# The alignment of the moving tiles against the weight tiles, modulo 512 bytes

## What is computed

```python
def first_block(x, ...):                   # 256 tokens
    h = h + rglru_mixer(rmsnorm(h, ...))   # linear recurrence, width 1280
    h = h + conv_ffn(rmsnorm(h, ...))      # 1024 -> 2 x 3072 -> 1024
    h = h + nsa_mixer(rmsnorm(h, ...))     # sparse attention, 16 heads
    h = h + conv_ffn(rmsnorm(h, ...))
    return rmsnorm(h, final_norm_g)

def second_block(x, c, ctx, ...):          # layer 0: x and ctx, layer 1: x alone
    for l in range(2):
        h = modulate(rmsnorm_2(x, norm1_g[l]), sh1, sc1)
        ...  = split_in(h @ w_in[l])
        x = x + g1 * merge(br_a, br_b, br_c, gates, w_out[l])
        x = x + g2 * swiglu(modulate(rmsnorm_2(x, ...), sh2, sc2), w_ffn_in[l], w_ffn_out[l])
    return rmsnorm_2(x, final_g)
```

## Time and profile before

| | |
|---|---|
| median of 3 runs | 2060.97 us (2057.18 to 2069.2) |
| the profiled execution | 2063.76 us |
| its span | 2062.0 us |
| TensorE matmuls, busy | 1983.8 us (96%), 12926 |
| TensorE weight loads, busy | 1752.5 us (85%), 12926 |
| VectorE, busy | 1506.9 us (73%) |
| ScalarE, busy | 896.6 us (43%) |
| mean granted clock of TensorE | 0.984 of full |

### The profile page before, as it was taken

The page is one execution under the profiler, slowest core; times in us unless marked ns, Lnnn a source line. Parts: engine busy times, 40 slices in busy tenths (PEclk is TensorE's granted clock), DMA queues, the critical chain, the costliest instruction groups (busy, mean ns, idle before and its releaser), DMA issues.

```text
span 2062.0 us, 33826 instructions
## 1 busy us (share of the span) xinstructions
PE 1983.8 (96%) x12926; PEld 1752.5 (85%) x12926; DVE 1506.9 (73%) x2738; ACT 896.6 (43%) x1436; POOL 360.5 (17%) x354
## 2 busy tenths in 40 slices
PE   7999999979999999989999999999999998998998
PEld 6999999859999988646888878888888866998998
DVE  7779887696987699776687667575666976675555
ACT  5744445473445432575343332222214356654443
POOL 0013333002325400001100312202231000013223
PEclk9999999899999999999999999999999999999999
DMA  7455565505555432103344325354563411554552
GB/s 260 165 199 190 195 257 192 181 2 224 192 184 211 166 116 82 41 1 114 133 182 180 116 82 204 143 204 166 202 223 133 143 42 42 184 186 162 185 203 83
DMA packets 46991, 318.14 MB, mean 154 GB/s; under 512 B 5008, under 2 KB 8080, under 8 KB 9488
## 3 DMA queue, kind: packets, MB, share of 16 engines
q1 hardware_dynamic: 45568, 309.58, 41.5%
q0 software_dynamic: 1296, 6.82, 1.0%
HBM read 315.33 MB, written 1.05 MB: 153 GB/s over the span
## 4 chain that ended last, share of the span: by engine, by line
PE 86%; DVE 7%; ACT 4%; issue 1%; POOL 1%; DMA 0%; DVEq 0%; ACTq 0%; POOLq 0%
PE ps L668 84%; ACT arena L1243 3%; PE ps L953 2%; DVE arena L2083 2%; DVE w_lo L1658 1%; DVE small L1888 1%; DVE arena L1910 1%; ACT w_hi L1243 1%; DVE ps L1877 1%; POOL arena L568 0%; ACT L1243 0%; POOL arena L564 0%; PE ps L1146 0%; DMA x<-x_in 0%; DVE arena L1640 0%
## 5 line engine op out<-in xcount | busy, mean ns | idle before, releaser
L668 PE MATMUL ps<-h_hi,w_hi 128*128 128x256 f32 (+2 forms) x2656 | 841.1, 317 | 17.3 <-DVE h_lo L1650 6.3
L668 PE MATMUL ps<-h_lo,w_hi 128*128 128x256 f32 (+2 forms) x2656 | 833.4, 314 | 0.0
L668 PE MATMUL ps<-h_hi,w_lo 128*128 128x256 f32 (+2 forms) x2656 | 833.3, 314 | 0.0
L1658 DVE TENSOR_TENSOR w_lo<-ring,w_hi 128x1024 fp32r<-128x1024 f32 x457 | 585.0, 1286 | 293.1 <-ACT w_hi L1243 292.2
L1243 ACT ACTIVATE w_hi<-ring 128x1024 fp32r<-128x1024 f32 x457 | 479.3, 1055 | 515.6 <-PE ps L668 481.2
L668 PEld LDWEIGHTS ps<-h_hi,w_hi 128*128 128x128 f32 (+1 forms) x2656 | 503.3, 189 | 55.0 <-issue 12.3
L668 PEld LDWEIGHTS ps<-h_lo,w_hi 128*128 128x128 f32 (+1 forms) x2656 | 504.8, 190 | 32.6
L668 PEld LDWEIGHTS ps<-h_hi,w_lo 128*128 128x128 f32 (+1 forms) x2656 | 503.1, 189 | 32.4
L1243 ACT ACTIVATE arena<-ps 128x512 f32<-128x512 f32 (+2 forms) x246 | 140.8, 579 | 344.7 <-PE ps L668 298.3
L668 PE MATMUL ps<-hid_hi,w_hi 128*128 128x256 f32 (+1 forms) x736 | 224.0, 304 | 0.0
L668 PE MATMUL ps<-hid_lo,w_hi 128*128 128x256 f32 (+1 forms) x736 | 224.0, 304 | 0.0
(11 more groups left out here) (193 smaller groups left out, 1945.3 us busy)
## 6 DMA issues: line engine op xcount, KB each, us to landing
ring<-wstream SPq DMA_DIRECT2D x290, 1024.0 KB, 4.8
arena<-c_in POOLq DMA_DIRECT2D x7, 512.0 KB, 4.0
arena<-rpb POOLq DMA_DIRECT2D x2, 1536.0 KB, 6.5
x<-x_in SPq DMA_DIRECT2D x2, 1024.0 KB, 12.1
out<-arena SPq DMA_DIRECT2D x8, 128.0 KB, 2.0
cst<-consts SPq DMA_DIRECT2D x1, 928.0 KB, 12.0
prm<-params SPq DMA_DIRECT2D x1, 580.0 KB, 10.7
ring<-wstream SPq DMA_DIRECT2D x1, 512.0 KB, 3.7
```

The costliest lines, as they stand in the source:

```text
L668: ins = nc.tensor.matmul(*a, **k)
L1658: V.tensor_tensor(w_lo[:, job % SPLITS, :], raw_job(job), w_hi[:, job % SPLITS, :].bitcast(F32), ALU.subtract).then_inc(weights_ready, 1)
```

## The change

It moves tiles and nothing else. No instruction is added, removed or put elsewhere.

```diff
-        h_at = {... for n, at in ((S, 48), (S2, 0))}
+        h_at = {... for n, at in ((S, 64), (S2, 0))}
...
+        sb("spacer", [P, 16])
         with nc.sbuf_tensor("arena", [P, ARENA], F32) as arena:
...
-            place("below_hi", 17104 - 15616, F32)
-            hi_rows = place("branch_hi", 48 + KC * S2)
-        branch_hi = {... for n, at in ((S, 48), (S2, 0))}
+            place("below_hi", 17088 - 15616, F32)
+            hi_rows = place("branch_hi", 64 + KC * S2)
+        branch_hi = {... for n, at in ((S, 64), (S2, 0))}
...
-        m_hidden = {... for n, at in ((S, 0), (S2, 16))}
+        m_hidden = {... for n, at in ((S, 0), (S2, 0))}
```

More of the change, by code:

```diff
@@ L310, in program @@
         h_rows = [sb(n, [P, KD * S2 + 128], F32R) for n in ("h_hi", "h_lo")]
-        h_at = {n: [v[:, at:at + KD * S2].rearrange("p (k t) -> p k t", t=S2) for v in h_rows] for n, at in ((S, 48), (S2, 0))}
+        h_at = {n: [v[:, at:at + KD * S2].rearrange("p (k t) -> p k t", t=S2) for v in h_rows] for n, at in ((S, 64), (S2, 0))}
         prm = sb("prm", [P, PARAM["end"]])
@@ L332, in program @@
             naq_lo, gq_lo = place("naq_lo", KC * S2), place("gq_lo", KC * S2)
-            place("below_hi", 17104 - 15616, F32)
-            hi_rows = place("branch_hi", 48 + KC * S2)
-        branch_hi = {n: hi_rows[:, at:at + KC * S2].rearrange("p (c t) -> p c t", t=S2) for n, at in ((S, 48), (S2, 0))}
+            place("below_hi", 17088 - 15616, F32)
+            hi_rows = place("branch_hi", 64 + KC * S2)
+        branch_hi = {n: hi_rows[:, at:at + KC * S2].rearrange("p (c t) -> p c t", t=S2) for n, at in ((S, 64), (S2, 0))}
         branch_lo = [v[:].rearrange("p (c t) -> p c t", t=S2) for v in (naq_lo, gq_lo, cy_lo)]
@@ L365, in program @@
         f_hidden = [v[:, 0:KF1 * S].rearrange("p (c t) -> p c t", t=S) for v in (hid_hi, hid_lo)]
-        m_hidden = {n: [v[:, at:at + KF1 * S].rearrange("p (c t) -> p c t", t=S2) for v in (hid_hi, hid_lo)] for n, at in ((S, 0), (S2, 16))}
+        m_hidden = {n: [v[:, at:at + KF1 * S].rearrange("p (c t) -> p c t", t=S2) for v in (hid_hi, hid_lo)] for n, at in ((S, 0), (S2, 0))}
         n_q = part(0, KD, S)
```

## The result

The changed kernel takes 2096.58 us, the median of six runs (2093.48 to 2099.25), against 2061.51 us for the kernel before in the same comparison (2055.46 to 2069.2). The ratio is 1.0176, with a 95% interval of 1.015 to 1.0201. Forecast were 2093.4 us and a step of +32.4 us; measured is +35.1 us between the medians, and +32.3 us between the two profiled spans, 2094.3 and 2062.0.

What follows compares the result with a forecast made beforehand. TensorE's matmul spacing was taken as the bound: 37.7 - 3.0 - 1.6 - 0.2 - 0.5 = +32.4 us on the median of 2060.97 us gave 2093.4 us, range 2046 to 2102 us.

Steps and rivals of the forecast that it cites:

- What bounds the kernel: Whole span: TensorE is 86% of the chain that ended last, so time is a count of matmuls times their spacing.
- The price at 256 bytes: Split 256-column tiles moved from 192 to 256 bytes would run at 120.0 ns, +37.7 us in all.
- How many ran at which spacing: Of 7,344 split 256-column matmuls before, 4,900 taken at 113.4 ns and 2,440 at 117.8 ns.
- The 512-column gains: Products going to 226.7 ns: layer 1's shared projections, nak, nav -1.6 us; nsa_v -0.2; layer 0 branch rests -0.5.
- Unsplit matmuls and the other engines: Unsplit float32 matmuls (lru, compression, nsa output) 0, bounds 2.2 us either way; attention, transposes, VectorE, ScalarE, GpSimd 0.
- What hides part of it: Longer spacings just before TensorE waits cost nothing; 3 us taken off the loss.
- the waits that I named: TensorE's waits at line 668: 6.3 and 4.4 us for h rests, 2.7 us for w_lo, where loss could hide.
- Rival 1: 256-column streams at 256 bytes always run at 113.3 ns: -13.3 us, 2047.7 us; chance 0.18.
- rival 3: All 256-column streams run at the long spacing, 117.8 ns: +17.3 us, 2078.3 us; chance 0.07.
- rival 4: No conflict left, 256-column streams fall to 108.1 ns: -50 us, 2011 us; chance 0.04.
- Rival 2: The address does not decide; the spacing mix stays, only 512-column gains may come: -2.3 us, 2058.7 us; chance 0.10.
- The rule against the forecast: Skill's two independent TensorE read ports: loading weights steals no read bandwidth, so address relations would not matter, 0 us.

Runs made afterwards that it cites:

- the two mirror images: Changed kernel with h alone back at 192 bytes: 2065.05 us, ratio 1.0036; kernel before with h of the 256-token stages at 0: 2083.4 us, ratio 1.0124.
- bare streams: Kernels of their own that only stream groups of 48 split matmuls, without the computation; 512 columns at 112 bytes gave 226.7 ns.

## Why the prediction was right

- **What bounds the kernel.** TensorE's busy time took the whole of the change, +33.1 us beside +32.3 us of span; reading spacings and not busy times was the right view, for a matmul is still shown 0.28 us long. Added up from start to start, the split 256-column matmuls take 920.6 us after 886.2, +34.4, where the forecast had 37.7 - 3.0 = +34.7.
- **The price at 256 bytes.** I took 120.0 ns, from the one place at 0, because 512 columns could not tell 0 from 256. Measured: 120.0 in every stage, and the period of 256 bytes is shown by 24 pairs. This was the step on which the forecast hung.
- **How many ran at which spacing.** Two thirds short and one third long held for the profiled execution, 4,860 and 2,262 of its means of three, and its span rose by 32.3 us. That the third is so large was chance: two thirds of it is the one stretch behind the pause at 517 us. The forecast counted the whole second ffn as long; its first 20 us were mostly short. For the typical execution it seems too many: the medians are 35.1 us apart and not 32.4, as they would be if the base were 2 to 3 us faster than its trace. With six runs each and a spread of 14 us in those of before, that remains an inference.
- **The 512-column gains.** The branch rests went from 229 to 226.7, 66.2 to 65.5 us from start to start, where 0.5 was forecast. Layer 1 gave less than the forecast 1.6 us: its h products went from 35.6 to 34.9 us, but the forecast took all 240 at 233.4, and half of nav had run at 229.2; nav in all took 24.3 us before and 24.5 after, as one pause in it grew. nsa_v gained 0.1 us, not 0.2.
- **Unsplit matmuls and the other engines.** 0 was right: 122 unsplit records in 26 us as in the earlier trace rows, and 215.9 ns at four addresses; VectorE and ScalarE are busy as long as before.
- **What hides part of it.** The 256-column spacings above 130 ns (starts of streams, pauses, stretches at the lower clock) hold 23.3 us beyond 115 ns each before, in 117 of them, and 20.1 us after, in 102. So the 3 us that I took off were there, but not where I had looked: the waits that I named, 6.3, 4.4 and 2.7 us, are 6.3, 4.4 and 2.5. Other pauses are shorter, among them the two above, and behind the pause before 1869 us, where the granted clock is 0.50, 16 matmuls run at the lower clock and not 26. The size was an estimate that happened to fit.
- **Rival 1** (256 is a good place) fell with the period; **rival 3** (117.8 everywhere) with the 120.0; **rival 4** with every row. **Rival 2** (not the address) is refuted as a whole by the two mirror images, but half of it is true: at 192 the start of the stream chooses between two spacings.
- **The rule against the forecast.** By the Trainium skill, "TensorE: Matmul & The Clock Gate", Step-by-step: what each phase is for, the next tile's weight load takes no read bandwidth from the running matmul, which would have given 0 us. This case's runs, with 113.3 to 122.2 ns for the same instructions at different distances of the two tiles, do not agree with it for split matmuls; for the unsplit ones, 215.9 ns at four addresses, they do. That the loss comes from the two reads meeting in the memory is how I explain it; the runs show its period and its dependence on the distance, and not the place where they meet.

## What to carry to other kernels

Where TensorE is the bound, measure the spacing from start to start in every stage and compare stages of the same shape; a difference of 3 to 6% at full clock with no idle time can be the distance between the moving tile and the weight tile. The good distance depends on the number of columns, so one place for all tiles lost here: 0 or 256 is best for 512 columns and among the worst for 256. 112 was always good for 256 columns, but for 512 only in bare streams, not in the whole kernel. Before choosing a distance, try it behind several different starts of the stream, since a single group can show a spacing that the real kernel does not keep.

## What had not been expected of the hardware

- A period of 256 bytes in the distance between moving and weight tile, exact to 0.1 ns over 24 pairs, in a kernel where no other engine works.
- Streams that settle in one of several spacings and stay there until a pause, once for 1,511 matmuls: 113.3 or 117.8 ns at 192 bytes, 116.7, 118.6 or once 113.3 at 144 (11 starts), always 113.3 at 112 (12 starts) and always 120.0 at 0 (9 starts).
- No split stream of 256 columns ran below 113.3 ns over 24 matmuls, although 122.2 ns was possible with the rounded part and the rest 112 bytes apart.
- The runs of before spread over more than those without the second state: 15 runs over 11.8 us, ten at 112 over 7.1 us, six of the changed kernel over 5.8 us. That the starts make the difference is not shown: the ten runs with h back at 192 spread over 7.7 us only.
